# A hybrid SSD, attention and conv-FFN layer on one core: half of the scan's x is turned by VectorE instead of TensorE

## The chip, the cores and the metric

The kernel runs on one NeuronCore of one Trainium2 chip. Its metric is the device time of one execution in microseconds (us), taken as the median of several runs. TensorE (PE in the profile, with its weight loads apart as PEld), VectorE (DVE), ScalarE (ACT), GpSimd (POOL) and the DMA queues of SyncE (SP) each work through a list of instructions of their own, and meet only at semaphores.

## The reference, cut to what matters

One decoder layer for 256 tokens and 2048 channels in float32: RMSNorm, one wide input projection, then a Mamba-2 (SSD) branch beside a sliding-window attention branch, merged by gates, an output projection, and a gated conv-FFN. The change lies in the SSD branch, which has 8 groups of 8 heads of 64 channels:

```python
xbc = jax.nn.silu(causal_dwconv(xbc, ssm_conv_w, ssm_conv_b))
xs, bm, cm = jnp.split(xbc, (D_INNER, D_INNER + SSM_GN), axis=-1)
...
x = (xh.astype(f32) * dt[..., None]).reshape(b, c, l, g, r, p)
cb = jnp.einsum('bclgn,bcsgn->bcgls', cc, bc)
y_diag = jnp.einsum('bcgls,bgrcls,bcsgrp->bclgrp', cb, decay, x)
...
y = y.reshape(b, s, SSM_GROUPS, gs) * jax.nn.silu(z.astype(f32)).reshape(b, s, SSM_GROUPS, gs)
y = y * lax.rsqrt(jnp.mean(y * y, axis=-1, keepdims=True) + NORM_EPS)
```

So each group needs its x with tokens on the partitions (to be summed over tokens), though the projection and the convolution leave it with channels on the partitions. And each group needs, for every token, the mean of y squared over its 512 channels.

## The kernel before

**Streaming of weights.** All projections work on weights that are streamed once from memory in units of 128x1024 floats (512 KB), through a ring of four slots. For each unit SP loads `raw`, ScalarE rounds it to `hi` (line 488), VectorE forms the rest `lo = raw - hi` (line 917), and TensorE multiplies both with the activations (lines 1534 and 1536 for results with channels on the partitions, 1519 to 1521 for the others). ScalarE may write a slot of `hi` when TensorE has used the unit four before. TensorE begins a unit when its `lo` is ready.

**The group phase.** After the keys and the dt unit come 8 groups of 20 units each (`G_UN = 20`, u = 0 to 19): 4 units for B and C, 8 for x and 8 for z, and after them 16 units (`X_UN`) of attention queries and gates. One unit is 16 matmuls of TensorE, and a group lasts 61 us. While the units of group g stream, the scan of group g-1 is done beside them. What is done after which unit is written out by hand in each engine's program: `ssd_side` for ScalarE and VectorE, `ssd_after` for TensorE. An engine works through its own list in order, so whatever stands ahead of a `lo` on VectorE delays that `lo`.

**The scan of one group, by the unit u of the next group** (before the change):
- u = 0, 1: VectorE copies the last group's roots to `rb` (line 1184, waits for GpSimd's root, line 427) and turns them in 16 small transposes of 32x64 (line 1189). ScalarE makes the drops of the decays.
- u = 2: ScalarE takes silu of all six tiles of the convolution, B, C and four of x, in one instruction (line 608, with a table load ahead). TensorE then makes C times B (lines 1706 and 1707) and turns x in 8 transposes of 128x128 into PSUM (line 1710).
- u = 3: VectorE scales the last group's y (line 1193).
- u = 5: ScalarE makes the exponentials; VectorE masks C times B (line 1147) and multiplies the turned x by dt out of PSUM into `xd` (line 1150).
- u = 8, 9: VectorE multiplies decays and C times B (line 1158), TensorE makes y behind unit 9 (lines 1721 and 1722).
- u = 12, 13: VectorE adds the skip and gates. u = 16: ScalarE squares y (line 640).
- u = 17: VectorE adds the four squares of each token with one reduce over a strided view (line 1175). TensorE makes the mean behind unit 16 (line 1728), VectorE adds eps at u = 19 (line 1180).

Beside the scan, at u = 2, 6, 10, 14 and 18 a finished pair of result banks is taken: ScalarE copies one half to `hb` (line 498), VectorE adds the other half and scales (lines 967 and 973), and for x, B and C the convolution follows one unit later (lines 602 and 1110).

Of the kernel before, what the change touches and what calls it, by code (L numbers as in the profile page):

```python
# [23 lines left out]
ALU = mybir.AluOpType  # L24
ACT = mybir.ActivationFunctionType
AX = mybir.AxisListType
ds = bass.ds

P = 128
SEQ = 256  # L30
TT = SEQ // P
# [3 lines left out]
SH, HD = 64, 64  # L35
G, NS = 8, 128
HG = SH // G
# [24 lines left out]
B32 = 32  # L62
# [42 lines left out]
def build(nc, x, params, w_in, w_ssm, w_attn, w_o, w_fi, w_fo, fnorm, out):  # L105
# [5 lines left out]
    with ExitStack() as ctx:  # L111
# [37 lines left out]
        x_tok, a = place("x_tok", [P, TT, D], region)  # L149
# [71 lines left out]
        def sem(name):  # L221
            return ctx.enter_context(nc.semaphore(name))
# [28 lines left out]
        sv_ready, z_scaled, rows_landed, rows_used = sem("sv_ready"), sem("z_scaled"), sem("rows_landed"), sem("rows_used")  # L251
        conv_first, conv_done, sz_ready = sem("conv_first"), sem("conv_done"), sem("sz_ready")
        decay_ready, x_turned, g_ready = sem("decay_ready"), sem("x_turned"), sem("g_ready")
        y_done, y_skipped, y_gated, y_squared = sem("y_done"), sem("y_skipped"), sem("y_gated"), sem("y_squared")
        y_summed, y_meaned, y_mean_ready, y_rstd = sem("y_summed"), sem("y_meaned"), sem("y_mean_ready"), sem("y_rstd")
        y_kept = sem("y_kept")
# [225 lines left out]
        def _(act):  # L482
# [122 lines left out]

            def silu_conv(k):
                act.wait_ge(conv_done, k * 3 + 3)
                act.activation(sv[:].rearrange("p a n -> p (a n)"), cv[:].rearrange("p a n -> p (a n)"),
                               ACT.Silu).then_inc(sv_ready, 1)

            def silu_gate(k):
                act.wait_ge(z_scaled, k * 2 + 2)
# [29 lines left out]
            def group(g, odd, it, body):  # L642

                def release(q):
                    act.wait_ge(pair_free[(A, B)[(5 * odd + q) % 2]], it * 5 + ((5 * odd + q) // 2 + J_G + 1))

                def second(q, done):
                    release(q - 1)
                    half_keep((A, B)[(5 * odd + q) % 2], done)

                for u in range(G_UN):
                    hi_of(U_G + u, g * G_UN)
                    if u == 2 and not (isinstance(g, int) and g == 0):
                        second(-1, g * G_UN + U_G)
                    if u in (6, 10, 14, 18):
                        second(u // 4 - 1, g * G_UN + (U_G + u // 4 * 4))
                    if u == 7:

                        conv_start(g * 3 + 1, ((4, g + 32), (5, g + 40)))
                    if u == 11:  # L660
                        conv_start(g * 3 + 2, ((0, g * 4), (1, g * 4 + 1)))
                    if u == 15:
                        conv_start(g * 3 + 3, ((2, g * 4 + 2), (3, g * 4 + 3)))
                    body(u)

            def ssd_side(k, u, at_squares=16):

# [245 lines left out]
        def _(ve):  # L913
# [203 lines left out]
            def gate_scaled_z(g, odd, it, j):  # L1117

                scaled(szb[:, 2 * j:2 * j + 2, :], (A, B)[(5 * odd + 3 + j) % 2], g * 5 + (H_G + 4 + j)).then_inc(z_scaled, 1)

            def group(g, odd, it, body):
                for u in range(G_UN):
                    lo_of(U_G + u, g * G_UN)
                    if u == 2 and not (isinstance(g, int) and g == 0):
                        gate_scaled_z(g - 1, 1 - odd, it, 1)
                    if u in (6, 10, 14):
                        conv_scaled((A, B)[(5 * odd + u // 4 - 1) % 2], g * 5 + (H_G + u // 4))
                    if u == 7:
                        conv_rest(g * 6, ((4, g + 32), (5, g + 40)))
                    if u == 11:  # L1130
                        conv_rest(g * 6 + 2, ((0, g * 4), (1, g * 4 + 1)))
                    if u == 15:
                        conv_rest(g * 6 + 4, ((2, g * 4 + 2), (3, g * 4 + 3)))
                    body(u)
                    if u == 18:
                        gate_scaled_z(g, odd, it, 0)

            def heads(t):
                return t.rearrange("p (h d) -> p h d", h=HG)

            def bc(t):
                return t[:, :, None].to_broadcast([P, HG, HD])

            def ssd_inputs(k):

                ve.wait_ge(x_turned, k + 1)
                ve.tensor_tensor(cbm[:].rearrange("p a n -> p (a n)"), ps[:, M, 0:3 * P],
                                 masks[:].rearrange("p a n -> p (a n)"), ALU.mult)
                for c in range(TT):
                    ve.tensor_tensor(heads(xd[:, c, :]), heads(ps[:, M + 1 + c, :]), bc(dtt[:, 0, c, ds(k * HG, HG)]),  # L1150
                                     ALU.mult)

            def ssd_blocks(k, half):
                if half == 0:
# [17 lines left out]

            def ssd_sum(k):
                ve.wait_ge(y_squared, k + 1)
                ve.tensor_reduce(ysum[:, :, None], ysq[:].rearrange("p i n -> p n i"), op=ALU.add, axis=AX.X) \
                    .then_inc(y_summed, 1)

            def ssd_mean(k):
                ve.wait_ge(y_meaned, k + 1)
# [20 lines left out]
            def ssd_side(k, u, at=STEPS, older=True):  # L1200
                if u == 0 and older:
                    ssd_spread(k - 1)
                    ve.drain()
                    ssd_root_rows(0)
                    ssd_root_rows(1)
                if u == 1 and older:
                    ssd_root_rows(2)
                    ssd_root_rows(3)
                if u == 3 and older:
                    ve.drain()  # L1210
                    ssd_scale(k - 1)
                if u == at["inputs"]:
                    ve.drain()
                    ssd_inputs(k)
                    ve.drain()
                if u == at["low"]:
                    ssd_blocks(k, 0)
                if u == at["high"]:
                    ssd_blocks(k, 1)
                if u == at["skip"]:  # L1220
                    ssd_skip(k)
                    ve.drain()
                if u == at["gate"]:
                    ssd_gate(k)
                if u == at["sum"]:
                    ssd_sum(k)
                if u == at["mean"]:
                    ssd_mean(k)
# [287 lines left out]
        def _(pe):  # L1516
# [184 lines left out]
            def turn_x(k, first=False):  # L1701

                pe.wait_ge(sv_ready, k + 1)
                if not first:
                    pe.wait_ge(y_skipped, k)
                pe.matmul(ps[:, M, 0:2 * P], sv[:, 4, 0:P], sv[:, 5, :], start=True, stop=True)
                pe.matmul(ps[:, M, 2 * P:3 * P], sv[:, 4, P:SEQ], sv[:, 5, P:SEQ], start=True, stop=True)
                for c in range(TT):
                    for i in range(4):
                        last = pe.transpose(ps[:, M + 1 + c, i * P:(i + 1) * P], sv[:, i, c * P:(c + 1) * P], ident[:])  # L1710
                last.then_inc(x_turned, 1)

# [227 lines left out]
```

## Time and profile before

| | |
|---|---|
| median of 3 runs | 1910.14 us (1909.37 to 1911.2) |
| profiled execution, its own time | 1909.57 us |
| its span, first to last instruction | 1907.8 us |
| granted TensorE clock | 0.999 |
| busy: TensorE matmuls, weight loads | 99%, 83% |
| busy: VectorE, ScalarE, GpSimd | 75%, 55%, 5% |

The table is read from the top: the span is what the engines need from the first to the last instruction, and 1.8 us lie around it. A matmul's end is modelled, so that two of them overlap in the records; how fast TensorE runs is read from the distance of their starts. A wait in brackets behind a row is idle time of that engine ahead of the row, and names what ended it.

### The profile page before, as it was taken

Reading aid. Unit: us, or ns where it says so; the run is one execution under the profiler, and the core shown is the slowest. Engines: PE = TensorE matmul, PEld = TensorE weight load, DVE = VectorE, ACT = ScalarE, POOL = GpSimd, SP = SyncE. Lnnn points to the kernel's source line nnn. Section 1 sums busy time; section 2 is a strip of 40 time slices with the busy share of each in tenths; the row PEclk is TensorE's granted clock in tenths of the full one; section 3 lists DMA queues with packets and bytes.
Section 4 is the critical chain, followed back from the end, with each engine's and each line's share of the span. In section 5 each row is a group of like instructions: output and inputs, shape, how many; then the busy total and the mean of one; then the engine's idle time right before and its main releaser. Section 6 shows DMA issues by size and latency. Waiting matters only on the chain.

```text
span 1907.8 us, 27178 instructions
## 1 busy us (share of the span) xinstructions
PE 1896.9 (99%) x9451; PEld 1583.3 (83%) x9451; DVE 1432.0 (75%) x1975; ACT 1050.6 (55%) x1434; POOL 89.7 (5%) x122
## 2 busy tenths in 40 slices
PE   9999999999999999999999999999999999999998
PEld 7888888888887778888888888888888888888886
DVE  6788898888979984645644778799899998964544
ACT  6567765677556664444344445556555556544443
POOL 1000000000012320000000000000100000000000
PEclk9999999999999999999999999999999999999999
DMA  7666666666654446666666565666666666665554
GB/s 249 198 189 176 197 191 193 190 176 198 196 167 133 132 154 193 195 188 198 195 191 196 188 234 177 207 190 194 188 192 195 195 197 188 205 210 191 196 191 142
DMA packets 249849, 361.55 MB, mean 190 GB/s; under 512 B 13168, under 2 KB 127920, under 8 KB 248368
## 3 DMA queue, kind: packets, MB, share of 16 engines
q1 hardware_dynamic: 249776, 360.59, 62.1%
q8 instruction: 44, 0.72, 0.2%
q14 instruction: 29, 0.24, 0.0%
HBM read 358.38 MB, written 2.16 MB: 189 GB/s over the span
## 4 chain that ended last, share of the span: by engine, by line
PE 69%; issue 30%; DVE 1%; POOL 0%; POOLq 0%; DVEq 0%; ACT 0%; ACTq 0%
PE ps L1519 21%; PE ps L1520 21%; PE ps L1521 21%; PE ps L1534 2%; PE ps L1536 1%; PE ps L1660 1%; PE ps L1671 0%; PE ps L1684 0%; DVE lo L917 0%; PE ps L1685 0%; DVE ysum L1189 0%; DVE acts L1193 0%; POOL rstd L427 0%; DVEq L1272 0%; DVE lg L1062 0%
## 5 line engine op out<-in xcount | busy, mean ns | idle before, releaser
L917 DVE TENSOR_TENSOR lo<-raw,hi 128x1024 fp32r<-128x1024 f32 x652 | 812.2, 1249 | 377.0 <-ACT hi L488 368.3
L488 ACT ACTIVATE hi<-raw 128x1024 fp32r<-128x1024 f32 x652 | 686.0, 1056 | 615.2 <-PE ps L1521 551.1
L1534 PE MATMUL ps<-uHL,hi 128*128 128x512 f32 x1536 | 544.6, 399 | 0.0
L1536 PE MATMUL ps<-uHL,lo 128*128 128x256 f32 x1536 | 428.7, 279 | 0.0
L1519 PE MATMUL ps<-hi,uHL 128*128 128x512 f32 x992 | 387.5, 391 | 0.7 <-DVE lo L924 0.7
L1521 PE MATMUL ps<-hi,uHL 128*128 128x512 f32 x992 | 386.1, 389 | 0.0
L1520 PE MATMUL ps<-lo,uHL 128*128 128x512 f32 x992 | 386.0, 389 | 0.0
L1534 PEld LDWEIGHTS ps<-uHL,hi 128*128 128x128 f32 x1536 | 288.4, 188 | 72.7 <-issue 5.4
L1536 PEld LDWEIGHTS ps<-uHL,lo 128*128 128x128 f32 x1536 | 289.4, 188 | 0.0
L1519 PEld LDWEIGHTS ps<-hi,uHL 128*128 128x128 f32 x992 | 186.2, 188 | 39.5 <-DVE lo L924 0.9
L1521 PEld LDWEIGHTS ps<-hi,uHL 128*128 128x128 f32 x992 | 186.2, 188 | 38.9
L1520 PEld LDWEIGHTS ps<-lo,uHL 128*128 128x128 f32 x992 | 186.3, 188 | 38.0
L1521 PE MATMUL ps<-hi,aL 128*128 128x512 f32 x384 | 149.5, 389 | 0.0
L1519 PE MATMUL ps<-hi,hH 128*128 128x512 f32 x352 | 136.9, 389 | 0.0
L1520 PE MATMUL ps<-lo,hH 128*128 128x512 f32 x352 | 136.9, 389 | 0.0
L1521 PE MATMUL ps<-hi,hL 128*128 128x512 f32 x352 | 136.9, 389 | 0.0
L1519 PE MATMUL ps<-hi,aHs 128*128 128x512 f32 x256 | 100.7, 393 | 0.0
L1520 PE MATMUL ps<-lo,aHs 128*128 128x512 f32 x256 | 99.6, 389 | 0.0
L1521 PEld LDWEIGHTS ps<-hi,aL 128*128 128x128 f32 x384 | 72.1, 188 | 15.2
L1418 DVE STREAM_TRANSPOSE gs<-gate_tok 32x256 f32<-32x256 f32 x176 | 76.8, 436 | 5.4 <-issue 1.7
L1418 DVE STREAM_TRANSPOSE ht<-value_tok 32x256 f32<-32x256 f32 x176 | 76.8, 436 | 5.4 <-issue 1.7
L1520 PEld LDWEIGHTS ps<-lo,hH 128*128 128x128 f32 x352 | 66.1, 188 | 13.8
(202 smaller groups left out, 1789.0 us busy)
## 6 DMA issues: line engine op xcount, KB each, us to landing
raw<-w_in SPq DMA_DIRECT2D x261, 512.0 KB, 3.9
raw<-w_ffn_in SPq DMA_DIRECT2D x176, 512.0 KB, 4.2
raw<-w_ffn_out SPq DMA_DIRECT2D x88, 512.0 KB, 4.4
raw<-w_ssm_out SPq DMA_DIRECT2D x64, 512.0 KB, 4.2
raw<-w_attn_out SPq DMA_DIRECT2D x32, 512.0 KB, 3.7
raw<-w_o SPq DMA_DIRECT2D x32, 512.0 KB, 4.4
rows_b<-cum_rows SPq DMA_DIRECT2D x8, 1024.0 KB, 6.8
x_tok<-x SPq DMA_DIRECT2D x8, 256.0 KB, 5.6
```

The costliest lines, as they stand in the source:

```text
L488: act.activation(hi[:, s % SLOTS, :], raw[:, s % SLOTS, :], ACT.Copy).then_inc(hi_ready, 1)
L917: ve.tensor_tensor(lo[:, s % SLOTS, :], raw[:, s % SLOTS, :], hi[:, s % SLOTS, :].bitcast(F32), ALU.subtract).then_inc(lo_ready, 1)
L1418: return ve.transpose(to[r * B32:(r + 1) * B32, :, :, q * B32:(q + 1) * B32], of[q * B32:(q + 1) * B32, :, :, r * B32:(r + 1) * B32])
L1519: pe.matmul(out, w[0], x[0], start=start, stop=False)
L1520: pe.matmul(out, w[0], x[1], start=False, stop=False)
L1521: return pe.matmul(out, w[1], x[0], start=False, stop=stop)
L1534: pe.matmul(ps[:, pair + c, :], w_hi, uHL[:, kk].rearrange("p a n -> p (a n)"), start=kk == 0, stop=False)
L1536: last = pe.matmul(ps[:, pair + c, 0:SEQ], w_lo, uHL[:, kk, 0, :], start=False, stop=kk == k - 1)
L1660: last = pe.matmul(ps[:, M + j, cols], qT[r, i, blk * P:(blk + 1) * P], kcur[r, keys], start=True, stop=True)
```

## The change

The program for x is split in two. Of the four channel tiles of x, tiles 0 and 1 become ready first (their convolution ends in the group itself at u = 11), tiles 2 and 3 at u = 15.

- ScalarE takes silu of tiles 0 and 1 apart, right after u = 17 of the same group (`silu_first_x`, behind the squares), and of the other four tiles at u = 2 of the next, as before.
- VectorE turns tiles 0 and 1 itself, `x_turn(g, q)` with q = 0 to 3: at u = 18 and 19 of the group and at u = 0 and 1 of the next. Each call is four stream transposes of 32 partitions by 2x2x32 elements, 16 for a group, from `sv` straight into `xd`.
- TensorE turns tiles 2 and 3 alone: 4 transposes for a group instead of 8.
- The multiplication by dt is split by tiles instead of by chunks: tiles 0 and 1 in place in SBUF, tiles 2 and 3 out of PSUM, each again 512 elements a partition.
- VectorE's second half of the root rows moves from u = 1 to u = 3, and the scaling of y from u = 3 to u = 4.
- The reduce over four squares becomes two adds, of 512 and of 256 elements a partition.

```diff
             def silu_conv(k):
                 act.wait_ge(conv_done, k * 3 + 3)
-                act.activation(sv[:].rearrange("p a n -> p (a n)"), cv[:].rearrange("p a n -> p (a n)"),
-                               ACT.Silu).then_inc(sv_ready, 1)
+                act.activation(sv[:, 2:6, :], cv[:, 2:6, :], ACT.Silu).then_inc(sv_ready, 1)
+
+            def silu_first_x(g):
+                act.wait_ge(conv_done, g * 3 + 2)
+                if not (isinstance(g, int) and g == 0):
+                    act.wait_ge(y_skipped, g)
+                act.activation(sv[:, 0:2, :], cv[:, 0:2, :], ACT.Silu).then_inc(sx_ready, 1)
...
                     body(u)
+                    if u == 17:
+                        silu_first_x(g)
...
                     body(u)
                     if u == 18:
                         gate_scaled_z(g, odd, it, 0)
+                        x_turn(g, 0)
+                    if u == 19:
+                        x_turn(g, 1)
...
+            def x_turn(g, q):
+
+                if q == 0:
+                    ve.wait_ge(sx_ready, g + 1)
+                src = sv[q * B32:(q + 1) * B32, 0:2, :].rearrange("p i (c n) -> p i c n", c=TT)
+                for j in range(P // B32):
+                    dst = xd[j * B32:(j + 1) * B32, :, 0:2 * P].rearrange("p c (i n) -> p i c n", i=2)
+                    ve.transpose(dst[:, :, :, q * B32:(q + 1) * B32], src[:, :, :, j * B32:(j + 1) * B32])
...
-                for c in range(TT):
-                    ve.tensor_tensor(heads(xd[:, c, :]), heads(ps[:, M + 1 + c, :]), bc(dtt[:, 0, c, ds(k * HG, HG)]),
-                                     ALU.mult)
+                for a, src in enumerate((xd[:, :, 0:2 * P], ps[:, M + 1:M + 3, 2 * P:4 * P])):
+                    dt = dtt[:, 0, :, ds(k * HG + a * (HG // 2), HG // 2)]
+                    ve.tensor_tensor(heads(xd[:, :, a * 2 * P:(a + 1) * 2 * P]), heads(src), bc(dt), ALU.mult)
...
-                ve.tensor_reduce(ysum[:, :, None], ysq[:].rearrange("p i n -> p n i"), op=ALU.add, axis=AX.X) \
-                    .then_inc(y_summed, 1)
+                ve.tensor_tensor(ysq[:, 0:2, :], ysq[:, 0:2, :], ysq[:, 2:4, :], ALU.add)
+                ve.drain()
+                ve.tensor_tensor(ysum[:], ysq[:, 0, :], ysq[:, 1, :], ALU.add).then_inc(y_summed, 1)
...
-                if u == 1 and older:
+                if u == 3 and older:
                     ssd_root_rows(2)
                     ssd_root_rows(3)
-                if u == 3 and older:
+                if u < 2:
+                    x_turn(k, 2 + u)
+                if u == 4 and older:
                     ve.drain()
                     ssd_scale(k - 1)
...
                 for c in range(TT):
-                    for i in range(4):
+                    for i in range(2, 4):
                         last = pe.transpose(ps[:, M + 1 + c, i * P:(i + 1) * P], sv[:, i, c * P:(c + 1) * P], ident[:])
```

On VectorE, from u = 18 of a group to u = 1 of the next, before the change (`lo` is the unit's own work, `szb` the taking of z, `ssum` the mean, `rb` and `ysum` the roots of the group before):

```order
L967 TENSOR_TENSOR szb<-ps,hb 128x512 [waits second_half_kept]
L973 TENSOR_TENSOR szb<-szb,rt 128x512
L917 TENSOR_TENSOR lo<-raw,hi 128x1024 [waits hi_ready]
L1180 TENSOR_SCALAR ssum<-ps 128x2 [waits y_meaned]
...
L917 TENSOR_TENSOR lo<-raw,hi 128x1024 [waits hi_ready]
L1184 COPY rb<-rstd 128x2x32 [waits y_rstd]
L1189 STREAM_TRANSPOSE ysum<-rb 32x2x32 x8
L917 TENSOR_TENSOR lo<-raw,hi 128x1024 [waits hi_ready]
L1189 STREAM_TRANSPOSE ysum<-rb 32x2x32 x8
```

And the same place after it (`xd<-sv` is the turn of x):

```order
L975 TENSOR_TENSOR szb<-ps,hb 128x512 [waits second_half_kept]
L981 TENSOR_TENSOR szb<-szb,rt 128x512
L1162 STREAM_TRANSPOSE xd<-sv 32x2x2x32 [waits first_x_ready]
L1162 STREAM_TRANSPOSE xd<-sv 32x2x2x32 x3
L925 TENSOR_TENSOR lo<-raw,hi 128x1024 [waits hi_ready]
L1201 TENSOR_SCALAR ssum<-ps 128x2 [waits y_meaned]
L1162 STREAM_TRANSPOSE xd<-sv 32x2x2x32 x4
...
L1205 COPY rb<-rstd 128x2x32 [waits y_rstd]
L1210 STREAM_TRANSPOSE ysum<-rb 32x2x32 x8
L1162 STREAM_TRANSPOSE xd<-sv 32x2x2x32 x4
L925 TENSOR_TENSOR lo<-raw,hi 128x1024 [waits hi_ready]
L1162 STREAM_TRANSPOSE xd<-sv 32x2x2x32 x4
```

Four batches of four transposes have come in, and the second batch of eight root transposes has left u = 1; it now stands behind the `lo` of u = 3.

On ScalarE, from u = 16 to u = 18, after the change (`ysq` are the squares; before it, the table load and `sv<-cv` stood at u = 2 of the next group, as one instruction of 128x1536):

```order
L646 ACTIVATE ysq<-y 128x1024 [waits y_gated]
L489 ACTIVATE hi<-raw 128x1024 [waits unit_used,raw_landed2]
L615 ACT_TABLE_LOAD [waits y_skipped]
L615 ACTIVATE sv<-cv 128x512 [waits conv_done]
L489 ACTIVATE hi<-raw 128x1024 [waits unit_used,raw_landed3]
L499 ACTIVATE hb<-ps 128x512 [waits unit_used,pair_b_free]
```

The table load has moved from u = 2 to u = 17, so their number is the same; one ACTIVATE for a group has become two.

## Rows read from the trace of the kernel before

**Rows 1.** The page, part 1: busy time, share of the span, instructions

```profile
PE 1896.9 (99%) x9451; PEld 1583.3 (83%) x9451; DVE 1432.0 (75%) x1975; ACT 1050.6 (55%) x1434; POOL 89.7 (5%) x122
```

**Rows 2.** Waits of TensorE's matmuls, longest of three: total, times, longest us

```profile
PE ps L1598 <- POOL ident L389: 1.6, 1, 1.6
```

**Rows 3.** Timeline, TensorE at the turn of x: start us, length us, what

```profile
226.93 1.04 PE L1710 MATMUL ps<-ident,sv 128*128 128x128 f32 x8
227.73 0.48 PE L1534 MATMUL ps<-uHL,hi 128*128 128x512 f32 x1
...
228.16 0.40 PE L1534 MATMUL ps<-uHL,hi 128*128 128x512 f32 x1
...
231.70 0.40 PE L1534 MATMUL ps<-uHL,hi 128*128 128x512 f32 x1
```

**Rows 4.** Windows, one group: length, busy us of PE, PEld, DVE, ACT, POOL

```profile
278.80:339.80 61.00, 61.00 (x371) 53.06 (x370) 53.60 (x84) 40.58 (x62) 1.60 (x1) 1.00 0.64 189
```

**Rows 5.** Waits of VectorE, window 278.8 to 339.8

```profile
DVE lo L917 <- ACT hi L488: 2.8, 2, 2.2
...
DVE rb L1184 <- POOL rstd L427: 0.6, 1, 0.6
```

**Rows 6.** Waits of VectorE, window 217.8 to 278.8

```profile
DVE lo L917 <- ACT hi L488: 3.1, 2, 2.1
...
DVE cbm L1147 <- PE ps L1710: 0.2, 1, 0.2
```

**Rows 7.** Waits of VectorE, window 400.7 to 461.7

```profile
DVE lo L917 <- ACT hi L488: 3.0, 2, 2.2
```

**Rows 8.** Groups by shape: line, engine, operation, count | busy us, mean ns

```profile
L1418 DVE STREAM_TRANSPOSE gs<-gate_tok 32x256 f32<-32x256 f32 x176 | 76.8, 436 | 5.4 <-issue 1.7
...
L1189 DVE STREAM_TRANSPOSE ysum<-rb 32x64 f32<-32x64 f32 x128 | 30.2, 236 | 2.3
...
L973 DVE TENSOR_TENSOR cs<-cs,rt 128x512 f32<-128x512 f32 x24 | 16.6, 692 | 2.2
...
L1175 DVE TENSOR_REDUCE ysum<-ysq 128x256 f32<-128x1024 f32 x8 | 16.2, 2023 | 0.0
...
L608 ACT ACTIVATE sv<-cv 128x1536 f32<-128x1536 f32 x8 | 11.9, 1491 | 0.1
```

**Rows 9.** Timeline, VectorE in the attention phase, a TENSOR_TENSOR of 256 elements a partition

```profile
576.87 0.42 DVE L1067 TENSOR_TENSOR lg<-lg 128x256 f32<-128x256 f32 x1
```

**Rows 10.** Timeline, VectorE in one group, from its `lo` of u = 1 on

```profile
274.91 1.97 DVE L1189 STREAM_TRANSPOSE ysum<-rb 32x64 f32<-32x64 f32 x8
...
283.37 1.23 DVE L917 TENSOR_TENSOR lo<-raw,hi 128x1024 fp32r<-128x1024 f32 x1 [0.59 <-ACT hi L488]
...
286.51 2.36 DVE L917 TENSOR_TENSOR lo<-raw,hi 128x1024 fp32r<-128x1024 f32 x2
...
292.87 1.22 DVE L917 TENSOR_TENSOR lo<-raw,hi 128x1024 fp32r<-128x1024 f32 x1 [2.16 <-ACT hi L488]
...
300.15 1.23 DVE L917 TENSOR_TENSOR lo<-raw,hi 128x1024 fp32r<-128x1024 f32 x1 [0.16 <-issue]
...
327.80 2.02 DVE L1175 TENSOR_REDUCE ysum<-ysq 128x256 f32<-128x1024 f32 x1
329.74 1.22 DVE L917 TENSOR_TENSOR lo<-raw,hi 128x1024 fp32r<-128x1024 f32 x1
```

**Rows 11.** Timeline, TensorE in the same group, at unit 8 and at the mean

```profile
301.46 0.40 PE L1534 MATMUL ps<-uHL,hi 128*128 128x512 f32 x1
...
302.50 0.39 PE L1534 MATMUL ps<-uHL,hi 128*128 128x512 f32 x1
...
330.84 0.50 PE L1728 MATMUL ps<-inv_w,ysum 128*128 128x1 f32 x4
```

**Rows 12.** Timeline, ScalarE in the same group, around unit 18

```profile
325.38 1.06 ACT L488 ACTIVATE hi<-raw 128x1024 fp32r<-128x1024 f32 x1 [0.32 <-PE ps L1536]
328.21 0.60 ACT L498 ACTIVATE hb<-ps 128x512 f32<-128x512 f32 x1 [1.77 <-PE ps L1536]
```

More of the change, by code:

```diff
@@ L253, in build @@
         decay_ready, x_turned, g_ready = sem("decay_ready"), sem("x_turned"), sem("g_ready")
+        sx_ready = sem("first_x_ready")
         y_done, y_skipped, y_gated, y_squared = sem("y_done"), sem("y_skipped"), sem("y_gated"), sem("y_squared")
@@ L1136, in group @@
                         gate_scaled_z(g, odd, it, 0)
+                        x_turn(g, 0)
+                    if u == 19:
+                        x_turn(g, 1)
             def heads(t):
-                return t.rearrange("p (h d) -> p h d", h=HG)
+                return t.rearrange("p c (h d) -> p c h d", h=HG // 2)
             def bc(t):
-                return t[:, :, None].to_broadcast([P, HG, HD])
+                return t[:, :, :, None].to_broadcast([P, TT, HG // 2, HD])
+            def x_turn(g, q):
[5 more added lines that the diff above has]
+                    ve.transpose(dst[:, :, :, q * B32:(q + 1) * B32], src[:, :, :, j * B32:(j + 1) * B32])
             def ssd_inputs(k):
```

## The prediction

> **What bounds the kernel now.** I read the page's busy shares first, then the waits of TensorE, then the windows and waits of one group. The reader is to see that TensorE is busy for 1896.9 of 1907.8 us [rows 1] and that its matmuls wait three times in all, 1.6 us at most and each time in the head of the program [rows 2]. So each matmul removed is time removed, as long as nobody makes TensorE wait. The question is who could. VectorE's 75% is a mean over the program; in one scan group it is busy for 53.60 of 61.0 us [rows 4]. What is left is no reserve as a whole. Most of it are gaps inside VectorE's own chains (the convolution's), which stay. What it could give up are its waits for others: 2.8 us for ScalarE's `hi` and 0.6 for GpSimd's root, 3.4 in this group [rows 5]; 3.1, the same 0.6 and 0.2 for TensorE, 3.9 in the one before [rows 6]; 3.0 and 0.6, 3.6, in a later one [rows 7]. Odd and even groups alternate between these figures.
>
> **How near VectorE is to TensorE.** The `lo` of unit 8 ends at 300.15 + 1.23 = 301.38 [rows 10], and TensorE begins that unit at 302.50 [rows 11]: 1.12 us of lead, the shortest of the group (unit 9 has the same).
>
> **The change part by part, for one group.**
>
> TensorE: eight transposes start at 226.93, and the matmul behind them at 227.73, of which about 0.03 is the first matmul's own step, so one takes 0.77 / 7 = 0.11 us [rows 3]. Four fewer are -0.44 us a group, and -3.5 us for 8 groups. Nothing else of TensorE changes.
>
> VectorE, the turn: no row has a transpose of 128 elements a partition. From both sides it is bound by 32x64 with 0.236 us and 32x256 with 0.436 [rows 8]. On the line between them, 64 elements above the lower end, it is 0.236 + 0.200 / 3 = 0.302; I take that, since both ends are the same operation on 32 partitions. To it comes 0.013 from one transpose to the next, since eight of 0.236 take 1.97, that is 7 steps of 0.248 and one of 0.236 [rows 8, 10]. 16 x 0.315 = 5.04 us. The ends are 16 x 0.248 = 3.97 and 16 x 0.449 = 7.18.
>
> What the batches do to their neighbours: two `lo` of 1.23 in a row take 2.36, so the second starts 0.10 before the first ends [rows 10], and transposes do not start early. The batches at u = 18 and 19 stand at new places, and each costs such an overlap: +0.20. The page VectorE: DVE Perf Modes of the Trainium skill, section Two Vector instructions with no wait between them, says why: an instruction whose output starts in another quarter of the partitions than the last output is held until everything before it has finished, and four in each batch change that quarter. The trace agrees (0.248 apart at 0.236 long). Without that hold the turn would be 16 x (0.302 - 0.10) = 3.2 us and VectorE would stay hidden.
>
> VectorE, the sum: the reduce of 2.02 gives way to the next `lo` after 329.74 - 327.80 = 1.94 [rows 10]. In its place stand an add of 512 elements, 0.692 [rows 8], a drain of some 0.09, and an add of 256, 0.42 [rows 9], less the overlap of 0.09: 1.11. -0.83 us.
>
> VectorE, the rest: the products with dt are again two of 512 elements; one input from SBUF instead of PSUM I cost at nothing (a tenth of a microsecond either way). Roots and scaling only move, by one or two units. What is queued behind them is each time one `lo`, whose lead is longer there than at unit 8. Sum for VectorE: 5.04 + 0.20 - 0.83 = +4.4 us a group.
>
> ScalarE: one ACTIVATE of 1.49 [rows 8] becomes one of 128x1024, about 1.06, and one of 128x512, about 0.60 [rows 12]: +0.2 us, and the table load only moves. At u = 17 silu and load put some 1.9 us ahead of the `hi` of unit 18, which started at 325.38. It then ends near 328.3, and VectorE comes to its `lo` at 329.74 - 0.83 = 328.9, so it is hidden; the copy at 328.21 waited 1.77 us for TensorE [rows 12]. At u = 2 ScalarE has 1.7 us less in front of the `hi` of unit 6, for which VectorE waited 2.16 us [rows 10]. That wait is what VectorE can now use. The new wait for `first_x_ready` at u = 18 ends long before VectorE gets there, near 327 against 331.
>
> SP issues nothing new, and GpSimd's root is asked for as before.
>
> **The balance.** +4.4 against 3.4 to 3.9 us of waits. VectorE becomes the bound of the group phase, by 0.5 to 1.0 us a group, and it meets TensorE at unit 8. Followed through:
> - Group 1 has longer waits (no root rows yet), so nothing is late there, and TensorE is 0.44 ahead of before.
> - Group 2: at its unit 6 VectorE is 4.4 - (0.58 + 0.59 + 2.16) = 1.1 behind its course [rows 5, 10], which itself began 0.44 earlier. Unit 8 is ready at -1.12 - 0.44 + 1.1 = -0.46 against TensorE's old start there, and TensorE would be there at -0.87, having saved two turns. It waits 0.41.
> - From there VectorE sets the pace. The five stretches from unit 8 of group 2 to unit 8 of group 7 have 3.9, 3.4, 3.9, 3.6 and 3.9 = 18.7 us of waits, and get 5 x 4.4 = 22.0 more work: +3.3, so +2.8 at unit 8 of group 7.
> - TensorE's last saving, -0.44 in the query units, is kept: +2.4.
> - The mean does not become a wait: the sum ended at 329.82 for a mean at 330.84, 1.0 of lead [rows 10, 11]; 1.1 of it goes and 0.83 comes back.
>
> The span goes from 1907.8 to 1910.2, and the profiled execution from 1909.57 to about 1912.0. The median of the runs shown, 1910.14, is 0.6 over that execution, and I forecast from the median: 1912.5 us, 0.13% slower. That is inside the 0.2% (3.8 us) within which a measurement of this kernel can't tell a change from none.
>
> The same page's section Rules for kernel authors speaks against the change as well: for a turn of 128x128 it names TensorE, if PSUM will do as the place. By rows, the four blocks cost 0.44 us on TensorE and 5.04 on VectorE. The rule asks for a loss, and the balance above says of which size.
>
> **The rivals.**
>
> *The cover holds.* If a transpose costs nearer to its lower end, VectorE adds 3.97 + 0.20 - 0.83 = 3.3 us, under the 3.4 free, and TensorE keeps its saving: 1910.14 - 3.5 = 1906.6. For it: 0.26 us instead of 0.302 would do on the mean of the groups, (3.7 + 0.63) / 16 - 0.013. Against it: both bounding rows have 0.2 us for 192 elements. In this case alone TensorE's own rhythm counts too. Ten pairs of matmuls from 228.16 to 231.70 take 0.354 each [rows 3], three from 301.46 to 302.50 take 0.347 [rows 11]; I see no wait that sets it, and four transposes fewer may swap which group gets which. With 160 pairs a group, half of the seven groups in each, that is up to 7 x 160 x 0.007 / 2 = 4 us either way: 1903 to 1910.
>
> *The free time can't all be used (the slower side).* The place is VectorE's wait for `hi` at the `lo` of unit 3 and for GpSimd's root. Once TensorE waits for VectorE at unit 8 and 1, ScalarE gets its slots later, since a `hi` needs the unit four before used up, and VectorE waits for ScalarE again: a circle of three engines instead of one. If 0.8 of the 3.7 us stay as waits, VectorE's excess is 1.5 instead of 0.7, and 5 x 0.8 = 4 us come on top: 1916.5. It is over 0.2% slower from 0.3 us a group on. For it: TensorE's lead at unit 8 falls to nothing. Against it: a unit takes 2.8 us and `hi` plus `lo` only 2.3, so ScalarE is about two units ahead. At the upper end of the transpose, 0.449, the same side holds: 7.18 + 0.20 - 0.83 = 6.5 a group, 5 x 6.5 - 18.7 = +13.8, and about +1.2 more by unit 8 of group 2: 1925. I give it little, as it would make 128 elements as dear as 256.
>
> *The change doesn't do what it says:* if the new first instruction of a batch waited for ScalarE. By the times above it has 4 us to spare.
>
> **How the numbers follow.** Forecast, VectorE the bound by 0.1 to 1.0 us a group: 0.47; its own range is 1909.5 to 1914.5, and nearly all of it is no change. The cover holds: 0.25, of which 0.10 is below 1906.3 by TensorE's rhythm. The slower side: 0.26. Something else: 0.02. So faster 0.10, same 0.62, slower 0.28. The range 1906.3 to 1916.8 leaves out the fast rhythm below and the dear transposes above.
>
> **What would show it.** Right: the turn's transposes at 0.30 us each; VectorE's waits for `hi` and for the root nearly gone in groups 3 to 7; TensorE with waits for `lo` at unit 8 of each of them, 0.5 to 1 us; and these groups 61.3 to 62 us long, group 1 at 60.6. Wrong: groups of 60.6 us to the end and no waits of TensorE (the cover holds), or waits of VectorE for `hi` that stay above 0.5 us a group beside waits of TensorE (the circle).

## The result, and the profile after it

The changed kernel takes 1913.47 us (median of 19 runs) against 1909.91 us for the kernel before (19 runs): ratio 1.0017, interval 1.0011 to 1.0024, so 3.6 us or 0.17% slower. The forecast was 1912.5 us. It called that a change that can't be told from none; the interval leaves out 1, so over 19 runs the loss is small but can be told. One of the 19 runs of the changed kernel took 3668 us, at a mean granted clock of 0.893, and stands apart from the other 18 (1912.3 to 1914.3).

The page of the kernel after, part 1, answers to [rows 1]:

```profile
PE 1895.9 (99%) x9419; PEld 1579.5 (83%) x9419; DVE 1463.6 (77%) x2111; ACT 1051.0 (55%) x1442; POOL 83.1 (4%) x122
```

TensorE is busy 1.0 us less in a span that is 3.8 us longer (1911.6). What has come in are waits of its matmuls, which answer to [rows 2] (total, times, longest, all in us; one wait in the head of the program, of 0.9 where it was 0.7, and one for a load, 0.5 in both, are not shown):

```profile
PE ps L1557 <- DVE lo L925: 4.1, 6, 1.1
...
PE ps L1694 <- DVE lg L1093: 0.5, 1, 0.5
```

Both lines are new: 4.1 us for `lo` in the group phase and 0.5 us in the attention. In the timeline (start, length), this is unit 8 of group 4 (VectorE's row is its `lo`), beside [rows 10, 11]:

```profile
301.79 0.28 PE L1559 MATMUL ps<-uHL,lo 128*128 128x256 f32 x1
303.17 0.50 PE L1557 MATMUL ps<-uHL,hi 128*128 128x512 f32 x1 [1.10 <-DVE lo L925]
```

```profile
301.89 1.23 DVE L925 TENSOR_TENSOR lo<-raw,hi 128x1024 fp32r<-128x1024 f32 x1 [0.17 <-issue]
```

The `lo` ends at 303.12 and TensorE goes on at 303.17. The lead of 1.12 us that it had before is gone.

The windows of groups 1 to 7 (length, then busy us of PE, PEld, DVE, ACT, POOL) answer to [rows 4]:

```profile
95.90:156.60 60.70, 60.70 (x366) 52.67 (x365) 54.26 (x87) 42.03 (x66) 0.70 (x1) 1.00 0.67 199
156.60:217.30 60.70, 60.70 (x366) 52.70 (x365) 55.87 (x97) 40.88 (x63) 0.69 (x1) 1.00 0.66 191
217.30:277.90 60.60, 60.60 (x366) 52.45 (x365) 55.74 (x94) 40.55 (x63) 0.69 (x1) 1.00 0.63 184
277.90:340.50 62.60, 61.23 (x366) 52.66 (x365) 57.91 (x102) 40.65 (x64) 0.69 (x1) 1.00 0.64 187
340.50:402.10 61.60, 60.88 (x366) 52.58 (x365) 56.51 (x95) 40.54 (x63) 0.69 (x1) 1.00 0.64 186
402.10:464.60 62.50, 61.28 (x366) 52.62 (x365) 57.82 (x102) 40.54 (x63) 0.69 (x1) 1.00 0.64 186
464.60:526.30 61.70, 60.89 (x366) 52.58 (x365) 57.24 (x99) 40.54 (x63) 0.69 (x1) 1.00 0.64 187
```

Before the change groups 1 to 4 and 6 were 61.0 us long and groups 5 and 7 60.9. Three groups are shorter now, together by 1.0, and four are longer, together by 248.4 - 243.8 = 4.6. That is +3.6 of the 3.8 us. In the short ones TensorE is busy from end to end; in the long ones 0.7 to 1.4 us are not.

The new operations by shape (count, busy us, mean ns) answer to [rows 8, 9]:

```profile
L1162 DVE STREAM_TRANSPOSE xd<-sv 32x128 f32<-32x128 f32 x128 | 38.7, 302 | 1.9
L1195 DVE TENSOR_TENSOR ysq<-ysq 128x512 f32<-128x512 f32 x8 | 5.5, 684 | 0.0
L1171 DVE TENSOR_TENSOR xd<-ps,dtt 128x512 f32<-128x512 f32 x8 | 5.5, 684 | 0.0
L1171 DVE TENSOR_TENSOR xd<-xd,dtt 128x512 f32<-128x512 f32 x8 | 5.5, 682 | 0.0
L1197 DVE TENSOR_TENSOR ysum<-ysq 128x256 f32<-128x256 f32 x8 | 3.4, 426 | 0.6
```

The transposes take the 302 ns of the forecast, and the product costs the same from SBUF as from PSUM (682 and 684). The waits of VectorE in groups 4 and 5, window 279 to 402, answer to [rows 5 to 7]. "Issue" marks time in which the engine waited for nothing that the profile shows:

```profile
DVE cv L1118 <- ACT cv L603: 2.4, 6, 0.5
DVE cv L1118 <- issue: 2.1, 12, 0.2
DVE lo L925 <- issue: 2.0, 9, 0.7
DVE acts L1214 <- issue: 0.6, 2, 0.3
```

The waits for `hi` (2.8 to 3.1 us a group) and for the root (0.6) are gone whole. What is left is marked "issue" (4.7 us in two groups), and the convolution's waits for ScalarE. In these two groups the kernel before has 4.0 us of "issue" as well. The largest of the issue gaps stands where VectorE's loop over pairs of groups turns, between groups 5 and 6; the second piece is the same place before the change:

```profile
397.36 0.15 DVE L1201 TENSOR_SCALAR ssum<-ps 128x2 f32<-128x2 f32 x1
397.55 1.25 DVE L1162 STREAM_TRANSPOSE xd<-sv 32x128 f32<-32x128 f32 x4
399.49 1.23 DVE L925 TENSOR_TENSOR lo<-raw,hi 128x1024 fp32r<-128x1024 f32 x1 [0.69 <-issue]
```

```profile
394.50 0.15 DVE L1180 TENSOR_SCALAR ssum<-ps 128x2 f32<-128x2 f32 x1
394.57 1.22 DVE L917 TENSOR_TENSOR lo<-raw,hi 128x1024 fp32r<-128x1024 f32 x1
396.36 0.20 DVE L1184 COPY rb<-rstd 128x64 f32<-128x64 f32 x1 [0.58 <-POOL rstd L427]
```

Before, the `lo` behind the loop's turn, where the program jumps back to the loop's first instruction, followed without a gap. Now VectorE stands idle for 0.69 us there, and for 0.47 at the turn before it, between groups 3 and 4. Once VectorE sets the pace, both count.

The wait for the root did not only get covered: the root itself became shorter. This is GpSimd at the same two places, after and before:

```profile
397.60 0.69 POOL L428 TENSOR_TENSOR rstd<-ssum,neghalf 128x2 f32<-128x2 f32 x1 [61.03 <-DVE ssum L1201]
```

```profile
394.73 1.60 POOL L427 TENSOR_TENSOR rstd<-ssum,neghalf 128x2 f32<-128x2 f32 x1 [59.50 <-DVE ssum L1180]
```

Before the change VectorE runs a `lo` beside it (394.57 to 395.79), now it runs transposes. In groups 1 to 7 every one of these roots took 1.60 to 1.61 us before and 0.69 to 0.70 after; the prediction had the root unchanged.

### The profile page after: what moved, and what is told of

The parts are those of the page before. It is cut to its first block, busy times and chain, and to the rows that moved or that the text cites. A ratio compares the mean times of both kernels' runs of the same rounds, so it can differ in the third digit from the quotient of the medians.

```text
span 1911.6 us, 27279 instructions
## 1 busy us (share of the span) xinstructions
PE 1895.9 (99%) x9419; PEld 1579.5 (83%) x9419; DVE 1463.6 (77%) x2111; ACT 1051.0 (55%) x1442; POOL 83.1 (4%) x122
## 4 chain that ended last, share of the span: by engine, by line
PE 69%; issue 30%; DVE 1%; POOL 0%; POOLq 0%; DVEq 0%; ACT 0%; ACTq 0%
PE ps L1542 21%; PE ps L1543 21%; PE ps L1544 21%; PE ps L1557 2%; PE ps L1559 1%; PE ps L1683 1%; PE ps L1694 0%; PE ps L1707 0%; DVE lo L925 0%; PE ps L1708 0%; DVE ysum L1210 0%; DVE acts L1214 0%; POOL rstd L428 0%; DVEq L1295 0%; DVE lg L1070 0%
## 5 line engine op out<-in xcount | busy, mean ns | idle before, releaser
L1544 PEld LDWEIGHTS ps<-hi,hL 128*128 128x128 f32 x352 | 66.1, 188 | 13.8
```

The lines of the kernel that those rows point to most:

```text
L1544: return pe.matmul(out, w[1], x[0], start=False, stop=stop)
```

## The experiments

The theory: VectorE's extra work is larger than the waits that it could give up, and all of it beyond them lengthens the groups, through `lo` at unit 8 and unit 1. The first four experiments test this and the first rival, the fifth tests the second. First rival: the time goes elsewhere (TensorE's own rhythm, the table load's new place, the sum). Second rival: the order of the new work, not its amount, costs the time. Intervals are those of the ratio to the kernel before on the same chip, whose median was 1909.8 to 1910.0 us. Differences from the kernel after are taken from its median of 1913.47 above, which comes from other runs.

**The sum alone** (in the kernel before):

```
- ve.tensor_reduce(ysum..., ysq..., op=ALU.add, axis=AX.X)
+ ve.tensor_tensor(ysq[:, 0:2, :], ysq[:, 0:2, :], ysq[:, 2:4, :], ALU.add)
+ ve.drain()
+ ve.tensor_tensor(ysum[:], ysq[:, 0, :], ysq[:, 1, :], ALU.add)
```

> The kernel before with the reduce over four squares replaced by the two adds, nothing else. Theory (TensorE sets the end of the kernel before, VectorE has 3.4 to 3.9 us of waits a group): VectorE gets 0.83 us shorter a group and the time does not move, 1909.9 within 1 us. Rival (the sum's end is what lets TensorE on): the mean comes 0.8 us earlier and the time falls by up to 7 x 0.8 = 5.6 us.

Measured: 1909.58 us, 0.9999 (0.9990 to 1.0008). VectorE is not the bound there, so 0.83 us less for it in each group buy nothing.

**The turn left out** (of the kernel after; the product reads tiles 0 and 1 unturned):

```
- for j in range(P // B32):
-     ...
-     ve.transpose(dst..., src...)
...
- for a, src in enumerate((xd[:, :, 0:2 * P], ...
+ for a, src in enumerate((sv[:, 0:2, :], ...
```

> The changed kernel without VectorE's 16 transposes a group: the product with dt reads tiles 0 and 1 unturned, everything else stays. Theory (the loss is VectorE's time alone): TensorE is the bound again and keeps its whole saving, 8 x 0.44 = 3.5 us under the kernel before, 1906.4, and 7 us under the changed kernel; no wait of TensorE for lo in the groups. Rival (the split silu or the moved root rows cost something of themselves, or TensorE's rhythm of 0.347 and 0.353 us a pair turns against it): it stays within 2 us of the kernel before. If TensorE's rhythm goes with the change as in its first groups (13 of 20 units slow instead of 10), 1 us of the 3.5 is lost.

Measured: 1907.42 us, 0.9987 (0.9978 to 0.9996); no wait of TensorE for `lo` in the group phase. So the 128 transposes cost 6.1 us of time, and everything else in the change gains 2.5. That is 1 us less than the 3.5 that four TensorE transposes a group amount to. The missing 1 us is in TensorE's rhythm: for whole units, its pairs of matmuls start either 0.347 or about 0.353 us apart. These are starts in group 3, first in this kernel, then in the kernel before; left out are two starts of pairs in the first piece and one in the second:

```profile
229.66 0.39 PE L1553 MATMUL ps<-uHL,hi 128*128 128x512 f32 x1
...
230.70 0.40 PE L1553 MATMUL ps<-uHL,hi 128*128 128x512 f32 x1
```

```profile
228.52 0.40 PE L1534 MATMUL ps<-uHL,hi 128*128 128x512 f32 x1
...
229.22 0.40 PE L1534 MATMUL ps<-uHL,hi 128*128 128x512 f32 x1
```

That is 1.04 us for three pairs here and 0.70 for two there, and over ten pairs 3.54 there [rows 3]. At this place this kernel is the faster one, but over a group it is the slower: before, on average half of the 20 units ran in either rhythm, and in this kernel 13 ran in the slower one. Three units of 8 pairs in 7 groups, at 0.006 us a pair, are the 1 us.

**The reduce kept** (in the kernel after, the edit of the first experiment undone):

> The changed kernel with the old reduce over the squares in place of the two adds. Theory (from group 3 on each microsecond of VectorE is a microsecond of the kernel): 0.83 us more for some 5 groups, and 0.8 us of the lead used up one group sooner, +4 to +5 us on 1913.5, so 1917.5 to 1918.5. Rival (VectorE has slack elsewhere, and the 3.6 us come from something else in the change): no more than 1 us on top.

Measured: 1918.78 us, 1.0046 (1.0033 to 1.0060): 5.3 us over the kernel after, 0.3 more than the theory's upper end. The waits of TensorE:

```profile
PE ps L1556 <- DVE lo L925: 6.9, 8, 1.2
```

The same edit is worth nothing where VectorE has slack and 5.3 us where it has none.

**Twelve transposes instead of 16** (one batch of four, that of u = 1, left out; that quarter of `xd` holds zeros, which GpSimd writes once ahead of the groups):

```
+ po.memset(xd[:], 0.0)
...
+ if q == 3:
+     return
```

> The changed kernel with 12 of the 16 transposes a group, the batch at u = 1 left out (xd holds zeros there). Theory (a threshold): VectorE's extra work is 4.4 - 1.26 = 3.1 us a group against 3.4 to 3.9 of waits, and with the 0.3 us a group that the loop's branch was seen to expose just about even; TensorE keeps most of its saving, 1906.5 to 1908. Rival (the price is proportional, a circle of waits rather than a threshold): three quarters of the way from 1906.4 to 1913.5, that is 1911.7.

Measured: 1907.50 us, 0.9986 (0.9977 to 0.9995).

```profile
PE ps L1562 <- DVE lo L928: 0.6, 2, 0.4
```

A quarter of the turn (1.26 us a group) takes back nearly all of its cost, not a quarter of it. The cost has a threshold, as the theory has it, and the rival's 1911.7 us is ruled out.

**The batch of u = 19 ahead of its `lo`** (the same instructions in another order):

```
  for u in range(G_UN):
+     if u == 19:
+         x_turn(g, 1)
      lo_of(U_G + u, g * G_UN)
```

> The changed kernel with the batch of u = 19 ahead of that unit's lo instead of behind the mean, so that a lo and the mean stand again in front of the loop's branch. In the changed kernel's trace the transposes there are followed by 0.67 us in which VectorE waits for nothing that the profile shows, once per turn of the loop (two groups). Theory (the branch is exposed by what stands ahead of it, and VectorE is the bound): that gap goes in the bound groups 4 and 6 and once more in the transition, 1.2 to 2 us less than the changed kernel, 1911.5 to 1912.3. Rival (the gap is the price of the branch wherever it stands): the time stays at 1913.5.

Measured: 1917.07 us, 1.0036 (1.0022 to 1.0049), 3.6 us over the kernel after; theory and rival both missed this. TensorE waits for `lo` 9 times, 6.6 us in all. VectorE at the start of group 5, and at the loop's turn behind it:

```profile
341.14 0.20 DVE L1205 COPY rb<-rstd 128x64 f32<-128x64 f32 x1 [0.58 <-POOL rstd L428]
...
401.56 0.15 DVE L1201 TENSOR_SCALAR ssum<-ps 128x2 f32<-128x2 f32 x1
402.48 1.23 DVE L925 TENSOR_TENSOR lo<-raw,hi 128x1024 fp32r<-128x1024 f32 x1 [0.76 <-issue]
```

The gap is still there, now behind the mean. And the wait of 0.58 for GpSimd's root, which the kernel after does not have, is back: no transposes stand between the mean and the copy of the root, and the root takes 1.60 us beside the `lo` again. From unit 8 of group 4 to that of group 5, and of 6 to 7, in which this wait lies, the kernel takes 0.54 and 0.58 us more than the kernel after. The order of the change is thus the better one of these two: its batch behind the mean hides the root.

**VectorE's loop written out** (the kernel after; same instructions, no loop on that engine):

```
- with ve.Fori(1, G // 2) as it:
+ for it in range(1, G // 2):
```

> The changed kernel with VectorE's loop over the groups written out (three turns of two groups), so that VectorE has no branch between groups 3 and 4 and between 5 and 6; the other engines keep their loops. Theory (part of the loss is VectorE's branch, which the transposes ahead of it expose by some 0.6 us, and VectorE is the bound): the gap goes, in 2 or 3 of the bound groups, 1 to 2 us less than the changed kernel, 1911.5 to 1912.5. If the register work of the loop was in the way as well, a little more. Rival (the gap belongs to the transposes or the mean): the time stays at 1913.5.

Measured: 1907.31 us, 0.9985 (0.9976 to 0.9994), 6.2 us less than the kernel after, where the theory had 1 to 2. VectorE's waits in the same two groups, then the loop's former turn, then group 3:

```profile
DVE cv L1118 <- ACT cv L603: 1.5, 6, 0.3
DVE lo L925 <- ACT hi L489: 0.5, 2, 0.3
DVE cv L1118 <- issue: 0.4, 1, 0.4
DVE ysum L1197 <- issue: 0.4, 1, 0.4
```

```profile
392.06 1.25 DVE L1162 STREAM_TRANSPOSE xd<-sv 32x128 f32<-32x128 f32 x4
393.33 1.23 DVE L925 TENSOR_TENSOR lo<-raw,hi 128x1024 fp32r<-128x1024 f32 x1
```

```profile
217.00:277.70 60.70, 60.70 (x366) 52.75 (x365) 57.14 (x99) 40.88 (x63) 0.69 (x1) 1.00 0.63 191
```

"Issue" falls from 4.7 to 0.8 us for two groups, the gap at the turn is gone, a little wait for `hi` is back, and TensorE waits for no `lo` in any group. So the loop took some 2 us of VectorE in each group, and without them VectorE has the time for the turn. With the turn at its full 5.0 us a group, the time is that of the kernel without the turn. What in the loop costs the 2 us stays open, and the kernel before was not run with its loop written out.

**Four more transposes on TensorE** (in the kernel before, behind `y_of`; their result is not read), on the rhythm:

```
+ for _ in range(4):
+     pe.transpose(ps[:, M + 3, 0:P], ident[:], ident[:])
```

> The kernel before with four more transposes of 128x128 a group on TensorE, behind y, whose result nobody reads: 7 or 8 x 0.44 = 3.3 us more by themselves, 1913.2. Theory on TensorE's rhythm (four transposes swap the pair's 0.347 and 0.353 us, as y does, so both together leave it as it is): one rhythm from group 1 to the end, 4 us more or 4 us less than 1913.2. Rival (the rhythm has nothing to do with it): half of the units in each as in the kernel before, 1913.2.

Measured: 1914.63 us, 1.0024 (1.0015 to 1.0033): +4.7, of which 8 x 0.44 = 3.5 is their own length. Both rhythms still occur in each group: the slow one from the mean on, through the turn of x, up to y, 13 of 20 units, which accounts for some 1 us of the remaining 1.2. Neither the theory (4 us either way) nor its rival (no change of rhythm) came out. In this kernel the rhythm changes behind y and behind the mean, in the kernel before behind y, with the turn left out behind the turn and behind y: in these three always where other matmuls stand between the units. What sets it stays open.

**Root without root transposes, twice.** VectorE's other transposes, 16 a group, only spread the root over the partitions. These experiments ask whether the turn of x pays once they are gone. A matmul with a 128x128 matrix of 1/512 gives the mean on all partitions, so that its root needs no turning. First GpSimd takes that root (`root_by_matmul`); the second kernel (`all_by_vector`) also turns all four tiles of x on VectorE.

```
- ve.tensor_scalar(ssum[:], ps[:, M + 3, SEQ:SEQ + TT], EPS, None, ALU.add)
- po.tensor_tensor(rstd[:], ssum[:], neghalf[:], ALU.pow)
+ ve.tensor_scalar(ysum[:], ps[:, M + 3, SEQ:2 * SEQ], EPS, None, ALU.add)
+ po.tensor_tensor(ysum[:], ysum[:], neghalf[:, 0:1].to_broadcast([P, SEQ]), ALU.pow)
```

> The changed kernel with the root rows taken from VectorE: TensorE makes the mean with a 128x128 matrix of 1/512, so that it stands on all partitions, VectorE adds eps to 256 elements, GpSimd takes the root of 256, and the 16 root transposes, the spread and their drains go (some 4.2 us of VectorE a group, 0.3 added). Theory: VectorE then needs 4.4 + 0.3 - 4.2 = +0.5 us a group beside 3.4 or more of waits, TensorE is the bound and keeps its saving as in the kernel without the turn: 1907 to 1907.5. Rival: GpSimd's root of 256 elements takes so long that the scaling of y at u = 4 waits for it (over 14 us), and the loss stays or grows; or TensorE's longer mean costs over 0.1 us a group.

> The kernel root_by_matmul with all four tiles of x turned by VectorE, in 16 transposes of 32x256 a group, and none by TensorE. By the kernel before's row of 0.436 us each, the turn takes 16 x 0.449 = 7.2 us instead of 5.04: VectorE has +2.7 us a group against the kernel before, still under its 3.4 of waits, but with the branch's 0.3 near it. TensorE saves 0.44 us a group more: theory 1903.5 to 1905, if the rhythm does not take a part. Rival: VectorE's lead at unit 8 is used up and the saving is given back, 1907 or more.

Measured: 2134.4 us, 1.1177 (1.1162 to 1.1193), and 2140.15 us, 1.1203 (1.1188 to 1.1219). The root in the first of them, by shape:

```profile
L428 POOL TENSOR_TENSOR ysum<-ysum,neghalf 128x256 f32<-128x256 f32 x8 | 329.9, 41234 | 432.8 <-DVE ysum L1203 432.8
```

It takes 41.2 us for 256 elements a partition, where 2 elements took 1.49 on average in the kernel before and 0.69 in the one after. These are VectorE's wait for it and TensorE's for VectorE:

```profile
DVE acts L1217 <- POOL ysum L428: 210.7, 7, 30.2
```

```profile
PE ps L1547 <- DVE lo L926: 172.2, 9, 25.0
```

TensorE also waits 38.9 us, once, for GpSimd in the attention. The rival on GpSimd's root is upheld, and neither kernel says anything of the turn.

Then ScalarE takes it (`root_by_scalar`): Sqrt at u = 19 with its own table load, and a reciprocal on VectorE before the scaling; and the same with all four tiles turned by VectorE (`all_by_vector_2`):

```
+ act.activation(ysum[:], ps[:, M + 3, SEQ:2 * SEQ], ACT.Sqrt, bias=rb[:, 1, 0:1])
+ ve.reciprocal(ysum[:], ysum[:])
```

> The changed kernel with the roots taken from VectorE and GpSimd: TensorE makes the mean on all partitions with a 128x128 matrix of 1/512, ScalarE the square root of 256 elements at u = 19 (one more table load there and one more at u = 2), VectorE the reciprocal of 256 elements in front of the scaling. VectorE loses 4.2 us of root transposes and spread and gets 0.3 to 2 us for the reciprocal, +0.5 to +2.3 a group against the kernel before, under its 3.4 of waits. Theory: TensorE is the bound, the mean costs it some 0.1 us more, 1907.4 to 1908.5. Rival (ScalarE's 3 us more a group delay the hi of units 19 to 3): waits of TensorE behind ScalarE, 1910 or more.

> The kernel root_by_scalar with all four tiles of x turned by VectorE in 16 transposes of 32x256, none by TensorE. TensorE saves 0.44 us a group more; VectorE gets 2.1 us more, +2.6 to +4.4 a group against the kernel before. Theory: if the reciprocal is cheap, VectorE stays under its waits and the time is 1904 to 1905.5; if it costs 2 us, VectorE is the bound again and the saving is given back, 1908 to 1910.

Measured: 1905.06 us, 0.9974 (0.9964 to 0.9984), and 1910.2 us, 1.0001 (0.9992 to 1.0010). By shape, the reciprocal in the first; then, of the second, its transposes by shape, and TensorE's waits:

```profile
L1220 DVE RECIPROCAL ysum<-ysum 128x256 f32<-128x256 f32 x8 | 14.0, 1753 | 0.7
```

```profile
L1169 DVE STREAM_TRANSPOSE xd<-sv 32x256 f32<-32x256 f32 x128 | 55.8, 436 | 2.1
```

```profile
PE ps L1553 <- DVE lo L930: 7.3, 7, 1.6
```

Without the root transposes VectorE has slack again, and TensorE waits for no `lo` in the groups of the first kernel. It is 2.3 us below the lower end of its expectation, and below the kernel with the turn left out, which has no wait for `lo` there either: its groups are 60.38 us long against 60.71. The rhythm gives most of that: 7 units of a group run in the slower one instead of 13, which is 6 x 8 x 0.006 = 0.29 us. The double turn (436 ns instead of 302, +2.1 us a group) uses it up, and the waits are back: the mechanism of the change a second time.

**All together** (`all_by_vector_2` with VectorE's loop written out):

> The kernel all_by_vector_2 with VectorE's loop over the groups written out. There VectorE set a pace of 61.2 to 61.6 us a group; writing the loop out took about 1.8 us of gaps from VectorE in the changed kernel, so it would need some 59.6. TensorE needs 60.38 us a group with the root by ScalarE and 0.44 less without its last four transposes, 59.9. Theory: TensorE is the bound again, the time is 1905.1 - 8 x 0.44 = 1901.6, plus or minus 1 by its rhythm. Rival: 0.3 us of room is too little and TensorE still waits at unit 8: 1903 to 1905.

Measured: 1902.52 us, 0.9960 (0.9946 to 0.9973), 7.5 us less than the kernel before and 11 less than the kernel after. TensorE's waits, and group 2:

```profile
PE ps L1553 <- DVE lo L930: 0.5, 1, 0.5
```

```profile
156.30:216.30 60.00, 60.00 (x360) 52.17 (x359) 56.92 (x82) 43.72 (x67) 0.00 (x0) 1.00 0.65 193
```

TensorE has no turn of x left and works through 60.0 us without a wait. How much of the 7.5 us is the second half of the turn is not told apart by a run: the same version with the turn split in halves was not run. `root_by_scalar` comes nearest, as it has the split turn and no wait for `lo` in the groups: 2.5 us lie between the two.

## Why the prediction was right, and where it was off

The forecast's mechanism is what happened: VectorE becomes the bound and meets TensorE at unit 8. Its rival on the slower side, the circle of waits, did not happen. Lengths from unit 8 to unit 8 of the next group, in us, from the starts of TensorE's matmuls (the last column is the prediction's difference):

| groups | before | after | difference | forecast |
|---|---|---|---|---|
| 1 to 2 | 60.55 | 60.71 | +0.16 | -0.02 |
| 2 to 3 | 61.41 | 60.78 | -0.63 | +0.5 |
| 3 to 4 | 60.56 | 62.28 | +1.72 | +1.0 |
| 4 to 5 | 61.40 | 61.73 | +0.33 | +0.5 |
| 5 to 6 | 60.57 | 62.49 | +1.92 | +0.8 |
| 6 to 7 | 61.40 | 61.70 | +0.30 | +0.5 |

- **TensorE, -3.5 us in all.** The size per transpose holds, but only 2.5 us arrived where VectorE was out of the way (`turn_left_out`). The rhythm, which the prediction kept for one rival, belongs into the forecast as well: from group 1 to 2 the kernel takes 60.71 us, without a wait, just as it does with the turn left out.
- **VectorE's +4.4 us.** Right in each term: 302 ns for 302, and the turn's cost for four transposes is 1.25, as 3 x 0.315 + 0.302 says. The rule cited from the Trainium skill (VectorE: DVE Perf Modes, Two Vector instructions with no wait between them) agrees with the trace: inside a batch they stand 0.315 apart. The prediction's "transposes do not start early" is too broad, though. The first one at u = 18, which starts in the same quarter as the instruction ahead of it, starts 0.08 before that one ends (333.24 against 332.63 + 0.69 in group 4). That the hold is the reason, and what the turn would cost without it, no run here tests. For the sum of the squares, the two adds are followed 0.76 and 0.34 us after their starts, 1.10 for 1.11. The overlaps lost at the two new places are 0.08 and 0.12, the forecast's 0.20.
- **The free time, 3.4 to 3.9 us a group.** Right in what goes: waits for `hi` and for the root fell to nothing from group 2 on, so no circle of three engines formed. Wrong in two sizes. First, the step "group 2: at its unit 6 VectorE is 1.1 behind its course" read group 4's waits for group 2. This is VectorE in the first window before the change that the prediction did not show, 156.8 to 217.8:

```profile
DVE lo L917 <- ACT hi L488: 4.0, 2, 2.1
...
DVE rb L1184 <- POOL rstd L427: 0.6, 1, 0.6
```

  With 4.6 us to give up, group 2 hid the whole turn, and VectorE met TensorE in group 3: its `lo` of unit 8 ends at 240.83 and TensorE begins at 240.89. TensorE waited from group 4 on, two groups later than forecast. Second, the prediction took the gaps inside VectorE's program as fixed. Two came in, at the loop's turns (0.47 and 0.69), in the two steps that came out 0.7 and 1.1 above the forecast. Take the two gaps off, and the four steps from group 3 to 7 are 61.81, 61.73, 61.80 and 61.70 us long, 61.8 on average; the forecast's steps, added to the lengths before, average 61.7. So VectorE's work was sized rightly, and the gaps are 1.16 of the 1.5 us that these groups took beyond the forecast. In `reduce_kept`, where VectorE has 0.83 us more to do, the same four are 62.7, 62.6, 62.7 and 62.6 without the gaps, 0.9 longer. The two errors partly cancel, which is luck: from group 3 to 7 it is +4.3 instead of +2.8, and at unit 8 of group 7 the kernel stood 3.2 us behind instead of 2.8.
- **The end, +3.8 instead of +2.4.** The query units were to keep -0.44. Between unit 8 of group 7 and the first of them 0.45 us were lost without a listed wait for `lo`, in a stretch where no instruction was added to TensorE. Two things add up there. With the turn left out the same stretch is 0.42 longer than before, by the rhythm alone. In the kernel after, only its last two units run slow (0.11 us), unit 8 itself takes 0.09 more, and 0.20 of the 0.45 lie around unit 16, where VectorE meets TensorE a second time:

```profile
514.37 0.28 PE L1559 MATMUL ps<-uHL,lo 128*128 128x256 f32 x1
514.53 0.50 PE L1557 MATMUL ps<-uHL,hi 128*128 128x512 f32 x1
```

  Its `lo` ends at 514.48, 0.05 ahead of that start. The prediction called the lead at unit 8 the shortest of the group, which holds for group 4; at unit 16 it was 1.12 to 1.36 before the change in groups 3, 5 and 7, the shortest of those groups, and is 0.05 or 0.06 now.
- **The attention.** Another 0.5 us is TensorE's new wait there, which the prediction did not have; its cause stays open.
- **"Most of it are gaps inside VectorE's own chains, which stay."** This sentence failed and it hid the cheap remedy. Some 2 us a group of such gaps come from the loop in the kernel after, as writing it out showed; the trace has them as "issue" ahead of `cv`, `lo` and `acts`.
- **The rule against the change** (the Trainium skill, VectorE: DVE Perf Modes, Rules for kernel authors: TensorE for a turn of 128x128 if PSUM will do as the place) agrees with the result as measured. It does not decide by itself: with VectorE's loop written out the same turn on VectorE costs nothing that can be seen (1907.31 against 1907.42 us without it).

## What to carry to other kernels

Where one engine is 99% busy, work moved off it pays only as far as the other engine's waits of that very group reach; read them for each group, since one with longer waits only delays the bound. An edit's worth changes with the bound: the same add was worth 0 and 5.3 us, and a quarter of the turn took back the whole loss. Before moving work, look at the gaps marked "issue" on the receiving engine: if it runs a loop, try it written out.

## What the runs showed of the hardware that was not expected

- A loop on VectorE over two groups of some 100 instructions each costs about 2 us a group: small gaps of 0.1 to 0.3 us, and 0.4 to 0.8 at its turn, which is counted in (in the kernel with twelve transposes 1.91 once, where VectorE had slack). The gap at the turn appeared with transposes ahead of it (0.69) and with the mean ahead of it (0.76), and not in the kernel before; why not there stays open.
- GpSimd's `pow` took 41.2 us for 128x256, VectorE's reciprocal 1.75 us, ScalarE's Sqrt 0.48 us beside a table load of 1.28. In the two kernels with the long `pow` TensorE's mean granted clock was 0.948 and 0.945, where the profiles of the other kernels show 0.998 or 0.999. In the first of the two TensorE stands idle for 22.8 us up to 194.15; the granted clock is 0.50, the level of 1.2 GHz, from 176 to 196 us and 1.00, that of 2.4 GHz, again from 200.
- GpSimd's `pow` of 128x2 took 1.60 us each time a `lo` of VectorE ran beside it for 1.05 us, and 0.69 to 0.72 each time one did not, in the kernel before, the one after and that with the batch ahead of its `lo`.
- The same pair of matmuls, in the same code, runs in steps of 0.347 or 0.353 us for whole units, at a granted clock of 1.00 in both.
